# Merged blocks written to the stage buffer inside the conformer branch, ahead of the output projection

## The reference

```
g_att, g_conv, g_sc = jnp.split(jax.nn.sigmoid(gate_in), N_BRANCH, axis=-1)
merged = (g_att * y_att + g_conv * y_conv + g_sc * y_sc) @ w_o
x = x + g1 * merged
h2 = modulate(rms_norm(x, ln2_g[l]), sh2, sc2)
x = x + g2 * swiglu(h2, w_ff1[l], w_ff3[l], w_ff2[l])
```

## Time and profile before

| | |
|---|---|
| median of 3 runs | 1278.47 us (1277.35 to 1278.88) |
| the profiled execution | 1276.72 us |
| its span | 1274.8 us |
| TensorE busy | 1230.0 us (96%) |
| VectorE busy | 879.2 us (69%) |
| ScalarE busy | 530.4 us (42%) |
| mean granted clock of TensorE | 0.989 |

### The profile page before, as it was taken

How to read it: one execution, slowest core, us unless ns; L and a number is a source line. 1 busy time by engine, 2 the same in 40 slices (tenths; PEclk the granted TensorE clock), 3 DMA queues, 4 the chain that set the end, 5 groups by cost and what they waited for, 6 DMA issues and landing times.

```text
span 1274.8 us, 19959 instructions
## 1 busy us (share of the span) xinstructions
PE 1230.0 (96%) x7460; PEld 1045.0 (82%) x7460; DVE 879.2 (69%) x1361; ACT 530.4 (42%) x891; POOL 57.1 (4%) x54
## 2 busy tenths in 40 slices
PE   6999999999998999999999999998999998999998
PEld 5767767677886888888888888888789888999997
DVE  5565677768776487678765566788788766666565
ACT  4432555522423353222222223446664554644444
POOL 2000000000000300000000000300000002000002
PEclk8999999999999999999999999999999998999999
DMA  9838212134453526547654754335343574666562
GB/s 298 248 122 250 77 51 67 34 79 120 112 169 116 165 67 193 170 147 215 188 182 160 228 168 133 102 101 135 86 132 92 143 214 117 195 183 193 171 175 89
DMA packets 281602, 187.67 MB, mean 147 GB/s; under 512 B 12795, under 2 KB 270129, under 8 KB 281521
## 3 DMA queue, kind: packets, MB, share of 16 engines
q1 hardware_dynamic: 281184, 186.42, 50.1%
q10 hardware_dynamic: 337, 0.15, 0.0%
HBM read 185.49 MB, written 1.05 MB: 146 GB/s over the span
## 4 chain that ended last, share of the span: by engine, by line
PE 86%; DVE 6%; ACT 3%; issue 3%; DVEq 0%; POOL 0%; ACTq 0%; POOLq 0%
PE bank L1816 21%; PE bank L1817 21%; PE bank L1818 21%; PE scores L2169 2%; PE bank L2152 2%; PE probsT L2178 2%; PE bank L2154 2%; PE bank L2153 2%; PE attended L2189 1%; ACT Whi L355 1%; PE bank L1851 1%; PE bank L1859 1%; DVE Wlo L366 1%; PE bank L1852 1%; PE bank L2242 1%
## 5 line engine op out<-in xcount | busy, mean ns | idle before, releaser
L1816 PE MATMUL bank<-Hhi,Whi 128*128 128x256 f32 (+1 forms) x1184 | 401.9, 339 | 3.4 <-DVE Wlo L366 3.4
L1817 PE MATMUL bank<-Hlo,Whi 128*128 128x256 f32 (+1 forms) x1184 | 397.6, 336 | 0.0
L1818 PE MATMUL bank<-Hhi,Wlo 128*128 128x256 f32 (+1 forms) x1184 | 397.5, 336 | 0.0
L366 DVE TENSOR_TENSOR Wlo<-Wraw,Whi 128x1024 fp32r<-128x1024 f32 (+3 forms) x318 | 317.4, 1010 | 108.8 <-ACT Whi L355 107.0
L355 ACT ACTIVATE Whi<-Wraw 128x1024 fp32r<-128x1024 f32 (+4 forms) x330 | 277.5, 862 | 155.5 <-PE bank L1818 99.2
L1816 PEld LDWEIGHTS bank<-Hhi,Whi 128*128 128x128 f32 x1184 | 224.9, 190 | 33.7 <-issue 7.7
L1817 PEld LDWEIGHTS bank<-Hlo,Whi 128*128 128x128 f32 x1184 | 225.0, 190 | 23.4 <-issue 1.2
L1818 PEld LDWEIGHTS bank<-Hhi,Wlo 128*128 128x128 f32 x1184 | 224.9, 190 | 23.0
L1816 PE MATMUL bank<-Uhi,Whi 128*128 128x256 f32 (+1 forms) x468 | 159.8, 341 | 0.7 <-DVE Ulo L1267 0.6
L1818 PE MATMUL bank<-Uhi,Wlo 128*128 128x256 f32 (+1 forms) x468 | 157.7, 337 | 0.0
L1817 PE MATMUL bank<-Ulo,Whi 128*128 128x256 f32 (+1 forms) x468 | 157.6, 337 | 0.0
(11 more groups left out here) (226 smaller groups left out, 1545.6 us busy)
## 6 DMA issues: line engine op xcount, KB each, us to landing
Wraw<-in_w_ff SPq DMA_DIRECT2D x120, 512.0 KB, 4.0
Wraw<-in_w_in SPq DMA_DIRECT2D x78, 512.0 KB, 3.9
ATT<-in_w_mod SPq DMA_DIRECT2D x58, 512.0 KB, 4.5
Wraw<-in_w_o SPq DMA_DIRECT2D x16, 512.0 KB, 4.2
ACC<-in_w_mod SPq DMA_DIRECT2D x14, 512.0 KB, 4.4
Wraw<-in_w_ff SPq DMA_DIRECT2D x16, 384.0 KB, 3.5
Wraw<-in_w_mla_o SPq DMA_DIRECT2D x8, 512.0 KB, 3.4
ATT<-in_w_mod SPq DMA_DIRECT2D x12, 256.0 KB, 6.3
```

Of the source, the lines that this page charges most:

```text
L366: last = eng.tensor_tensor(lo, raw, hi.bitcast(F32), ALU.subtract)
L1816: pe.matmul(dst, sh, mh, start=j == 0, stop=False)
L1817: pe.matmul(dst, sh, ml, start=False, stop=False)
L1818: last = pe.matmul(dst, sl, mh, start=False, stop=j == k - 1)
```

## The change

ACT and DVE make the pieces of two merged blocks inside the branch: those of group i-1's blocks stand behind group i, the last two behind the last group. Blocks 0 to 6 go to blocks 2 to 8 of `Uhi` and `Ulo`, whose earlier contents have been read by then. Block 7 still goes to `Hhi[7]`, `Hlo[7]`, and it alone keeps ACT's wait for the last gate tile. TensorE reads the operands through the function `merged(k)`; its order of matmuls is the same.

```
--- before.py
+++ after.py
@@ -366,6 +366,10 @@
                     last = eng.tensor_tensor(lo, raw, hi.bitcast(F32), ALU.subtract)
                 last.then_inc(lo_done[slot], 1)
             at.chunk.next()
+
+        def merged(k):
+
+            return (Uhi[:, SO0 + k, :], Ulo[:, SO0 + k, :]) if k < DT - 1 else (Hhi[:, k, :], Hlo[:, k, :])
 
         NS = [2, 1]
         half = [slice(s * SEQ, (s + 1) * SEQ) for s in range(2)]
@@ -1004,14 +1008,20 @@
                 group(mean_squares)
                 group(lambda: root(TQ, CH))
                 normalised()
-                for _ in range(4):
+                def merged_out(i):
+
+                    for k in (2 * i, 2 * i + 1):
+                        if k == DT - 1:
+                            act.wait_ge(tile_done, at.tiles.now() - 2)
+                        t = outs[DT + k]
+                        act.wait_ge(drained[t.bank], t.drained)
+                        operand(merged(k)[0][:, 0:TQ], G[:, k, 0:TQ], z=False, scale=0.5)
+
+                for i in range(4):
                     group()
-
-                act.wait_ge(tile_done, at.tiles.now() - 2)
-                for k in range(DT):
-                    t = outs[DT + k]
-                    act.wait_ge(drained[t.bank], t.drained)
-                    operand(Hhi[:, k, 0:TQ], G[:, k, 0:TQ], z=False, scale=0.5)
+                    if i:
+                        merged_out(i - 1)
+                merged_out(3)
 
                 def residual_squares(m):
                     t = at.tile()
@@ -1661,10 +1671,17 @@
                 last.then_inc(conv_s, 1)
                 for j in range(2):
                     low(Ulo[:, CO0 + j, 0:TQ], ACC[:, j, 0:TQ], Uhi[:, CO0 + j, 0:TQ], scale=0.5)
+                def merged_low(i):
+
+                    for k in (2 * i, 2 * i + 1):
+                        hi, lo = merged(k)
+                        low(lo[:, 0:TQ], G[:, k, 0:TQ], hi[:, 0:TQ], scale=0.5)
+
                 for i in range(4):
                     group(i)
-                for k in range(DT):
-                    low(Hlo[:, k, 0:TQ], G[:, k, 0:TQ], Hhi[:, k, 0:TQ], scale=0.5)
+                    if i:
+                        merged_low(i - 1)
+                merged_low(3)
 
                 def residual(m, mod):
 
@@ -1818,27 +1835,34 @@
                     last = pe.matmul(dst, sl, mh, start=False, stop=j == k - 1)
                 return last
 
+            def normed(k):
+
+                return Hhi[:, k, :], Hlo[:, k, :]
+
+            def stage(k):
+
+                return Uhi[:, k, :], Ulo[:, k, :]
+
             def gemm(slot, width, col, m, k, ops, o0, n, ready=None):
 
                 t = new_tile()
-                oh, ol = ops
 
                 def terms(j):
                     a = j * width + col
-                    return (Whi[:, slot, a:a + m], Wlo[:, slot, a:a + m],
-                            oh[:, o0 + j, 0:n], ol[:, o0 + j, 0:n])
+                    hi, lo = ops(o0 + j)
+                    return Whi[:, slot, a:a + m], Wlo[:, slot, a:a + m], hi[:, 0:n], lo[:, 0:n]
 
                 last = split_product(banks[t.bank][0:m, 0:n], k, terms, ready)
                 return t, last
 
-            H, O = (Hhi, Hlo), (Uhi, Ulo)
+            H, O = normed, stage
 
             def tile_of(m, k, ops, o0, n, ready=None, width=None):
 
                 _, last = gemm(chunk(), width or m, 0, m, k, ops, o0, n, ready)
                 last.then_inc(tile_done, 1)
 
-            def tiles_together(slots, ns, ready, before={}, inside={}):
+            def tiles_together(slots, ns, ready, before={}, inside={}, ops=normed):
 
                 tiles = [new_tile() for _ in slots]
                 for j in range(DT + 1):
@@ -1848,27 +1872,27 @@
                         pe.wait_ge(op_hi, ready + j + 1)
                         for t, slot, n in zip(tiles, slots, ns):
                             w, dst = slice(j * P, (j + 1) * P), banks[t.bank][:, 0:n]
-                            pe.matmul(dst, Whi[:, slot, w], Hhi[:, j, 0:n], start=j == 0, stop=False)
-                            pe.matmul(dst, Wlo[:, slot, w], Hhi[:, j, 0:n], start=False, stop=False)
+                            pe.matmul(dst, Whi[:, slot, w], ops(j)[0][:, 0:n], start=j == 0, stop=False)
+                            pe.matmul(dst, Wlo[:, slot, w], ops(j)[0][:, 0:n], start=False, stop=False)
                     if j in inside:
                         inside[j]()
                     if j:
                         pe.wait_ge(op_lo, ready + j)
                         for t, slot, n in zip(tiles, slots, ns):
                             w, dst = slice((j - 1) * P, j * P), banks[t.bank][:, 0:n]
-                            last = pe.matmul(dst, Whi[:, slot, w], Hlo[:, j - 1, 0:n], start=False, stop=j == DT)
+                            last = pe.matmul(dst, Whi[:, slot, w], ops(j - 1)[1][:, 0:n], start=False, stop=j == DT)
                             if j == DT:
                                 last.then_inc(tile_done, 1)
 
             def half_product(t, slot, k, ops, s, a, b, ready):
 
-                oh, ol = ops
                 for j in range(a, b):
                     pe.wait_ge(op_lo, ready + j + 1)
                     w, dst = slice(j * P, (j + 1) * P), banks[t.bank][:, half[s]]
-                    pe.matmul(dst, Whi[:, slot, w], oh[:, j, half[s]], start=j == 0, stop=False)
-                    pe.matmul(dst, Whi[:, slot, w], ol[:, j, half[s]], start=False, stop=False)
-                    last = pe.matmul(dst, Wlo[:, slot, w], oh[:, j, half[s]], start=False, stop=j == k - 1)
+                    hi, lo = ops(j)
+                    pe.matmul(dst, Whi[:, slot, w], hi[:, half[s]], start=j == 0, stop=False)
+                    pe.matmul(dst, Whi[:, slot, w], lo[:, half[s]], start=False, stop=False)
+                    last = pe.matmul(dst, Wlo[:, slot, w], hi[:, half[s]], start=False, stop=j == k - 1)
                 return last
 
             def seam_tiles(k, ops, ready):
@@ -1925,17 +1949,17 @@
                 slots.append(chunk())
                 tiles.append(new_tile())
                 if third_whole:
-                    half_product(tiles[2], slots[2], DT, (Hhi, Hlo), 0, 0, DT, ready)
+                    half_product(tiles[2], slots[2], DT, H, 0, 0, DT, ready)
                     together(1, slots, tiles)
                 else:
-                    half_product(tiles[2], slots[2], DT, (Hhi, Hlo), 0, 0, DT - 1, ready)
+                    half_product(tiles[2], slots[2], DT, H, 0, 0, DT - 1, ready)
                     together(1, slots[:2], tiles[:2])
-                    half_product(tiles[2], slots[2], DT, (Hhi, Hlo), 0, DT - 1, DT, ready).then_inc(tile_done, 1)
-
-            def first_tiles(ns, ready, before={}, inside={}):
+                    half_product(tiles[2], slots[2], DT, H, 0, DT - 1, DT, ready).then_inc(tile_done, 1)
+
+            def first_tiles(ns, ready, before={}, inside={}, ops=normed):
 
                 slots = [chunk() for _ in ns]
-                tiles_together(slots, ns, ready, before, inside)
+                tiles_together(slots, ns, ready, before, inside, ops)
 
             def total(n, count):
 
@@ -2285,12 +2309,12 @@
                 at.operand.n += DT
                 if l == 0:
                     at.ring = 0
-                first_tiles((TQ,) * 2, o)
+                first_tiles((TQ,) * 2, o, ops=merged)
                 for j in range(2, WHOLE if l == 0 else DT):
-                    tile_of(P, DT, H, 0, TQ, o)
+                    tile_of(P, DT, merged, 0, TQ, o)
                 if l == 0:
                     mod_turn(2)
-                    context_total = seam_tiles(DT, H, o)
+                    context_total = seam_tiles(DT, merged, o)
                 else:
                     at.square.n += DT
                     total(TQ, DT)
```

## The result

Six runs of each kernel, side by side: the change takes a median of **1270.96 us** (1270.57 to 1271.47), the kernel before 1278.56 (1277.35 to 1279.52). The ratio is 0.9944, with a 95% interval of 0.9934 to 0.9954. Forecast were 1272.2 and 6.3 us of gain; the medians give 7.6, the ratio 7.2 with an interval of 5.9 to 8.4, which holds the 6.3. The changed kernel's profiled execution took 1270.57, its span is 1268.8.

The account below looks back on a forecast made before the run. TensorE, busy 1230.0 of 1274.8 us, bounds the kernel; gains of 4.26 us in layer 0 and 2.03 in layer 1, together 6.3, off the median 1278.47 give 1272.2 us, range 1269.8 to 1274.8.

Parts of the forecast that it names:

- rival (a): Layer 1's stall also costs a slow clock stretch in executions behind the median, which goes too: 1270.4 us, chance 0.15.
- The stalls: Output projection start: waits for low pieces vanish, 2.19 and 1.71 us; first matmul earlier by 0.28 and 0.32 (layers 0, 1).
- The clock in layer 0: Behind layer 0's stall, 40 matmuls take 10.85 instead of 9.06 us at slow clock; 1.79 us comes back.
- The stretch near 827: Seam near 827, granted clock 0.72, comes 4.3 us earlier; slow stretches elsewhere might gain, within a rival of chance 0.08.
- What the inserted work costs: Early pieces on DVE and ACT inside the branch of both layers cost nothing on the path, because of idle times.
- the idle time before layer 0's gate split: DVE's idle 3.13 us before the split at 381.42 takes up 1.22 us of low pieces, shrinking to 1.9.
- that for the fold: Layer 0, at 389.14: TensorE's 1.24 us wait for DVE's fold isn't moved, as DVE's idle 3.13 absorbs the inserted 1.22.
- the 1.75 between the two: Median 1278.47 lies 1.75 us above the profiled execution's 1276.72, taken as about one slow stretch of the clock.

Follow-up runs that it names:

- the buffer alone: The change's stage buffer without the early pieces, all made behind the last group, against the kernel before: 1277.96 us, ratio 0.9998.
- high pieces early: The change with ACT's high pieces early but DVE's low pieces all behind the last group, against the kernel before: 1277.98 us, ratio 0.9999.
- The filled stall: The kernel before plus nine unread matmuls between the eighth and ninth joint matmul of layer 0: 1274.81 us, ratio 0.9976.
- the second comparison: The unaltered changed kernel run once more beside the kernel before: 1270.39 us, ratio 0.9939.
- the filled kernel: The kernel before plus unread matmuls in both layers' idle time at the output projection's start (2 and 9, 13 and 14): 1275.34 us, ratio 0.9978.
- layer 1 alone: The change with its early pieces in layer 1 only, against the kernel before: 1273.98 us, ratio 0.9970.
- layer 0 alone: The change with its early pieces in layer 0 only, against the kernel before: 1271.85 us, ratio 0.9949.
- three times the work: The change with DVE making each of the four low pieces inside the branch three times: 1272.40 us, ratio 0.9950 against the kernel before.
- layer 1 filled: The kernel before plus fourteen unread matmuls between the eighth and ninth joint matmul of layer 1: 1277.30 us, ratio 0.9991.
- the version with the split start: The change with TensorE beginning the output projection on the first output block alone: 1268.82 us, ratio 0.9917 against the kernel before.

## Why the prediction was right

The time lies in the range, the direction is right, and the mechanism is the one forecast. The measured 1270.96 lies nearer to rival (a)'s 1270.4 than to the forecast of 1272.2, so the clock gave more than the sum had. Step by step:

**The stalls.** Forecast 2.19 + 0.28 in layer 0 and 1.71 + 0.32 in layer 1. The handovers of the changed profile give 4.19 in layer 0 together with the clock (forecast 4.26) and 2.10 in layer 1 (2.03). With the clock up before and after, layer 0 is 14.22 against 11.67, so 2.55 without the clock against 2.47. These terms were right to a tenth: 4.65 us together, 4.5 forecast.

**That it hangs on the low piece**, and not on the buffer or the high pieces: shown by the buffer alone and by high pieces early, both without a gain.

**The clock in layer 0.** Forecast 1.79, measured 15.86 - 14.22 = 1.64 between profiles. The filled stall shows the cause: with the idle time filled and nothing else changed, the stretch is gone and the kernel faster. The idleness doesn't always bring it: of five profiles with layer 0's stall whole, four have handovers of 15.8 to 15.9, the one with the buffer alone 14.2.

**The term that was too small** is the clock, for which the sum had 1.8, layer 0's stretch alone. What is left of the measured 7.2 (5.9 to 8.4) behind the 4.65 of idle time is 2.6 (1.3 to 3.8), and 3.1 by the ratio of the second comparison; the filled kernel gives 2.8 (1.7 to 4.0) on its own. The mean granted clock of each execution says the same: on the mean 0.9890 in the 58 executions of the kernel before beside the experiments, 0.9915 in the eleven of the change. That difference of 0.0025 over 1276 us is 3.2 us, an estimate that takes TensorE as busy in the slow stretches. So it is some 3 us of clock, about 1 more than the sum had; the near ends of the intervals still allow 1.8.

Where the excess sits isn't settled. Layer 1's stall, set at nothing because its one row showed 1.00, is one place; rival (a) had it. The gain with layer 1 alone (2.6 to 5.0 against 2.0 to 2.1 of idle time) speaks for it, and of the profiles with that stall unfilled three have granted clocks of 0.83, 0.76 and 0.66 there and handovers of 10.6, 12.0 and 11.8, and two (the kernel before, and high pieces early) have none, with handovers of 9.5. The stretch near 827, 1.5 us, is the other: the gain with layer 0 alone (4.7 to 8.2 against 4.3) is above the forecast though layer 1's stall stays. It is not shown to be that stretch; how often a slow one follows the stall of layer 1 could differ in that kernel too. By the Trainium skill ("TensorE: Matmul & The Clock Gate", Part 1) the number of slow matmuls varies between runs of one kernel; the profiles agree as far as they go: the same code in layer 1 took 9.54 in the kernel before and 11.77 in the one with layer 0's stall filled.

**What the inserted work costs.** Nothing in the change, as forecast: from 300 us to layer 0's handover, with the inserted pieces in between, TensorE's distance from the kernel before stays the same to 0.01 us, and the idle time before layer 0's gate split fell by 1.20, as forecast. The lag of a group, which the account of idle times took for needed in layer 1, is not. With three times the work two waits of TensorE grew: in layer 0 that for the fold, by 0.4, by way of DVE's queue, which the prediction named; in layer 1 that for the second output block's weights, by 0.6, perhaps by way of SP's load behind DVE's split, which it did not count.

**The profile against the median.** The prediction took the 1.75 between the two for one slow stretch at one place. The parts vary more than that: the start up to layer 0's handover took 398.2 in the profile before and 399.5 after, up to 401.4 in others, and the stretch between the handovers 625.5 and 624.1. No other profile has a shorter start than that of the kernel before, so part of the 1.75 may be the start, which the change doesn't touch. The forecast took the gain read from one execution off the median of others. That this fits to 1.3 us is in part luck: read from an execution like that of the buffer alone, with the clock up behind layer 0's stall and down behind layer 1's, the parts would have come out otherwise.

Left open: how much of the gain between the handovers (1.4 us) belongs to the change. The slow stretch near 860, which the changed profile has and that of the kernel before has not, costs nothing that can be read: profiles with and without it take 624.0 to 624.4 us there. The one near 827 makes the difference. Three profiles have it and take 625.5: the kernel before, layer 1 alone, and high pieces early. All three have layer 0's stall, but so do the kernels with the buffer alone and with layer 1 filled, which haven't got it; and the three are also those with the shortest starts, 398.2 and 398.3 us against 399.5 and more. In how many executions of the kernel before it comes, no run shows. Open too is whether the version with the split start leaves anything to a split of the third block's weights.

## What to carry to other kernels

Make the operands of a product as its inputs are finished, ahead of the last producer, where the feeding engines have idle time; a buffer whose old contents have been read makes that possible. A short stall of the matrix engine can cost most of its length again in clock behind it (1.6 us behind 2.5 here), and in some executions only: one profile that shows the clock up does not price it, so fill the stall with matmuls that nobody reads and time that kernel. When operands come early, look again at orders that were made to hide their lateness; here taking two blocks together had become the next wait.

## What the runs showed of the hardware that I had not expected

- In layer 0, idle times of 0.53 and 2.03 us were followed by a granted clock of 0.57 over 4 us in the kernel before, and by 1.00 in the kernel with the buffer alone, with the same idle times. In layer 1 idle times of 1.62 and 1.55 did not lower it, nor did 1.35 and 1.82; 2.60 and 0.43 did, 1.96 and 0.94 and a single 2.91 did more. The length of the idle time alone doesn't tell which.
- Extra matmuls made the kernel faster: 38 of them, 2.8 us less by the ratio (1.7 to 4.0).
- Two executions of one kernel can differ by more than the stalls are worth: 1271.3 and 1276.96 us with early pieces in layer 0 alone. In the slower one's profile layer 1's handover is 2.4 us longer than in the kernel before.
- The shape of a stall can hang on a load: in layer 1 the high pieces came late where ACT waited for the third output block's weights, 1.41 us in one profile, 1.10 in another, not at all in the kernel before.
